# Residual rows turned for the router, token lists in halves, and seven and eight weight buffers in a two-layer hybrid decoder step

## The reference

```python
def hier_moe(h, w_group, b_group, w_router, b_router, w_gate, w_up, w_down):
    x2 = h.reshape(m, d)                       # rms_norm(residual) * gain
    g_logits = x2 @ w_group + b_group
    g_w, g_idx = lax.top_k(jax.nn.softmax(g_logits, axis=-1), 1)
    e_in = (x2 @ w_router + b_router).reshape(m, N_GROUPS, E_PER_GROUP)[jnp.arange(m), g_idx[:, 0]]
    top_v, top_i = lax.top_k(e_in, TOP_K_INNER)
    top_w = jax.nn.softmax(top_v, axis=-1) * g_w
    combine = ...                              # top_w at the two chosen experts of each row
    for e in range(N_EXPERTS):                 # 16 experts, D_FF_E = 512
        hid = jax.nn.silu(x2 @ w_gate[e]) * (x2 @ w_up[e])
        y = y + combine[:, e:e + 1] * (hid @ w_down[e])
```

## Time and profile before

| | before |
|---|---|
| median of 3 runs (lowest, highest) | 1469.57 us (1468.09, 1473.25) |
| the profiled execution: time, span | 1469.94 us, 1468.2 us |
| mean granted clock of TensorE, share of full | 0.948 |
| busy share of the span: PE, PEld, DVE, ACT, POOL | 90%, 51%, 39%, 21%, 13% |
| moved by DMA, mean rate | 341.06 MB, 232 GB/s |
| expert weights, issued at line 533 | 96 loads of 2 MB |

### The profile page before, as it was taken

One profiled execution on the slowest core, in us unless ns is written; L12 is line 12 of the kernel. 1 busy time (PEld: TensorE's weight loads), 2 busy tenths in 40 slices (PEclk: granted clock), 3 DMA queues, 4 the chain that ended last, 5 costly groups with the idle time before them and its releaser, 6 DMA issues. The chain is left out here.

```text
span 1468.2 us, 27307 instructions
## 1 busy us (share of the span) xinstructions
PE 1318.9 (90%) x10905; PEld 741.6 (51%) x10906; DVE 577.3 (39%) x1435; ACT 304.2 (21%) x783; POOL 185.4 (13%) x469
## 2 busy tenths in 40 slices
PE   7999999999599999887899998889995999998990
PEld 3444456544365456554643444556543655555550
DVE  2159944443423111111658995665216131111115
...
GB/s 283 193 132 58 147 315 314 340 123 131 182 324 264 393 376 403 405 409 359 105 0 58 33 115 116 116 116 73 216 72 174 196 320 366 397 391 402 403 268 205
DMA packets 87597, 341.06 MB, mean 232 GB/s; under 512 B 25843, under 2 KB 33107, under 8 KB 73506
## 3 DMA queue, kind: packets, MB, share of 16 engines
...
## 5 line engine op out<-in xcount | busy, mean ns | idle before, releaser
L1265 PE MATMUL banks<-arena 128*32 128x128 f32 (+1 forms) x4736 | 358.2, 334 | 26.7 <-issue 13.7
L1265 PEld LDWEIGHTS banks<-arena 128*32 128x32 f32 (+1 forms) x4736 | 238.9, 126 | 145.3 <-issue 52.5
L1293 PE MATMUL banks<-arena 128*64 128x512 f32 (+1 forms) x1184 | 173.1, 492 | 1.1 <-ACT arena L1755 1.1
L1861 DVE TENSOR_TENSOR arena<-arena,banks 128x256 f32<-128x256 f32 (+5 forms) x84 | 38.5, 459 | 272.1 <-PE banks L1265 176.8
L940 PE MATMUL banks<-arena 128*128 128x512 f32 x320 | 141.1, 595 | 1.2 <-DMA arena<-in_wstream 1.1
L2233 DVE COPY arena<-banks 128x256 f32<-128x256 f32 (+1 forms) x56 | 21.4, 382 | 295.8 <-PE banks L1278 289.5
L1861 DVE TENSOR_TENSOR arena<-banks,arena 128x512 f32<-128x512 f32 (+5 forms) x159 | 70.6, 473 | 124.4 <-ACT arena L1677 84.5
L1168 PE MATMUL banks<-arena 128*128 128x512 f32 x256 | 115.6, 610 | 3.6 <-ACT arena L1795 2.3
L968 PE MATMUL banks<-arena 128*128 128x512 f32 x256 | 116.5, 600 | 0.0
L1755 ACT ACTIVATE arena<-banks 128x512 f32<-128x512 f32 (+1 forms) x56 | 29.6, 528 | 363.2 <-PE banks L1293 363.2
L1293 PEld LDWEIGHTS banks<-arena 128*64 128x64 f32 (+1 forms) x1184 | 58.6, 123 | 84.4 <-issue 70.0
...
## 6 DMA issues: line engine op xcount, KB each, us to landing
...
```

Of the source, the lines that this page charges most:

```text
L1265: last = mm(bank(b, 0, 4 * n, n * j, n * j + n), x[:, c, :], w[:, c, 4 * n * j:4 * n * j + 4 * n], start=(c == 0), stop=(c == DC - 1))
L1293: last = mm(bank(3, 0, 8 * n, n * q, n * q + n), ht2[g % 2][:, 128 * i + n * j:128 * i + n * j + n], w[:, c, 8 * n * q:8 * n * q + 8 * n], ...
L1861: return v.tensor_tensor(out, x, y, op)
```

## The change

Four things change together.

- **Buffers.** The sets of three become one ring of seven slots in layer 0 and eight in layer 1: the three ring buffers, the three of `over_w`, then `WORK` 0 to 4096, and in layer 1 `QT` 0 to 4096. Block n goes to slot n mod 7 (8), and waits for the last product with block n-7 (n-8). `WORK` held the normed rows `hn`, so SP's loop waits for their transfers too.
- **Residual rows turned.** Norms 1 and 3 join `SCALED_LATER`: TensorE turns `h` itself, one job earlier in the order, and VectorE scales the logits. `hn` is still made, for the gathers, the last two tiles of it after all tiles are in `xt`. ScalarE's first copy of router sums moves ahead of its last root, and its load of the Exp table behind the copies.
- **Routing.** The weights of the choice go behind the lists (`choice_weights`); `slot_of` is made in two halves, each with its signal; the lists are copied and cast ahead of keys and rank.
- **First expert.** Its rows are copied in two halves, the first as soon as four of eight turns are done, and its gate product waits for the halves one by one.

Some semaphores are merged (`lf_dve`, `lf_act` to `lf`; `ln_var`, `ln_root`, `ln_done` to `ln`), with the same order.

```diff
-SCALED_LATER = (2,)
+SLOTS = (7, 8)
+SCALED_LATER = (1, 2, 3)
...
-    slots = [[[ring[2], ring[0], ring[1]], over_w], [[ring[1], ring[2], ring[0]], over_w]]
+    slots = [[ring[i] for i in first] + over_w + [at(*wide) for wide in more]
+             for first, more in (((2, 0, 1), [("WORK", 0, 4096)]), ((1, 2, 0), [("WORK", 0, 4096), ("QT", 0, 4096)]))]
...
+    def slot_of_block(l, s, i):
+
+        return slots[l][(3 * s + i) % SLOTS[l]]
+
+    def block_landed(l, s, i):
+
+        n = 3 * s + i
+        return f"weights{l}_{n % SLOTS[l]}", 16 * (n // SLOTS[l] + 1)
+
+    def block_used(l, s, i):
+
+        before, j = divmod(3 * s + i - SLOTS[l], 3)
+        name = ("gate_mm", "up_mm", "down_mm")[j] + str(l)
+        return name, upto(name, ENDS[before])
+
...
             sp.wait_ge(S(f"ranked{l}"), upto(f"ranked{l}", 1))
+            sp.wait_ge(S(f"hn_out{l}_0"), upto(f"hn_out{l}_0", 48))
+            sp.wait_ge(S(f"hn_out{l}_1"), upto(f"hn_out{l}_1", 32))
             for s in range(2, NE):
                 k = sp.value_load(block_i[0:1, s:s + 1], min_val=0, max_val=3 * NE - 3)
-                for i, name in enumerate((f"gate_mm{l}", f"up_mm{l}", f"down_mm{l}")):
-                    sp.wait_ge(S(name), upto(name, ENDS[s - 2]))
+                for i in range(3):
+                    if 3 * s + i >= SLOTS[l]:
+                        name, count = block_used(l, s, i)
+                        sp.wait_ge(S(name), count)
                     sp.wait_ge(S("x_in_0"), 16)
                     weights(l, s, i, a["wstream"][bass.ds(k + (b + i), 1)].rearrange("a p w -> (a p) w"))
 
...
                     last.then_inc(S(f"out_mm{l}"), 1)
+                    if b == 1 and t >= 1:
+                        turn_h(2 * l + 1, t - 1)
                     if b == 1 and t >= 2:
-                        turn_h(2 * l + 1, t - 2)
-                    if b == 1 and t >= 3:
-                        route_strips(l, t - 3)
-            turn_h(2 * l + 1, 3)
-            route_strips(l, 2)
+                        route_strips(l, t - 2)
             turn_h(2 * l + 1, 4)
             route_strips(l, 3)
             route_folds(l, (0, 1, 2), 1)
...
-            pe.wait_ge(S(f"placed{l}"), upto(f"placed{l}", 1))
             for n in range(2 * NT):
+                if n % NT == 0:
+                    pe.wait_ge(S(f"placed{l}"), upto(f"placed{l}", n // NT + 1))
                 last = mm(bank(5, 0, NE), slot_of[:, n, :], tok_of[:, n, :], start=(n == 0), stop=(n == 2 * NT - 1))
             last.then_inc(S(f"list_mm{l}"), 1)
...
+                if s == 0 and c == 3:
+                    last.then_inc(S(f"xg_used{l}"), 1)
...
+            def first_tokens(c):
+                if c % 4 == 0:
+                    pe.wait_ge(S(f"xgt{l}"), upto(f"xgt{l}", c // 4 + 1))
+
             pe.wait_ge(S(f"tok{l}"), upto(f"tok{l}", 1))
             turn_x(l, 0)
...
-                part_features(0, g3(slots[l][s % 2][0], DC), x, n).then_inc(S(f"gate_mm{l}"), 1)
+                part_features(0, g3(slot_of_block(l, s, 0), DC), x, n, first_tokens if g == 0 else None)\
+                    .then_inc(S(f"gate_mm{l}"), 1)
...
                 square(t)
+                if n % 2 and t == NT - 1:
+                    route_part(n // 2, 0)
                 if n in (2, 4):
                     if t:
...
+            route_part(l, 1)
+            route_part(l, 2)
             af(tick[2], tick[2], ACT.Exp)
...
                 if b == 1 and t >= 1:
-                    mean_square(2 * l + 1, t - 1)
-                    inverse_root(2 * l + 1, t - 1)
-                    normed(2 * l + 1, t - 1)
-                if b == 1 and t >= 2:
-                    to_xt(2 * l + 1, t - 2)
+                    to_xt(2 * l + 1, t - 1)
+                if b == 1 and t < NT - 1:
+                    mean_square(2 * l + 1, t)
+                    inverse_root(2 * l + 1, t)
+                if b == 1 and t < NT - 2:
+                    normed(2 * l + 1, t)
+            to_xt(2 * l + 1, NT - 1)
             mean_square(2 * l + 1, NT - 1)
-            to_xt(2 * l + 1, NT - 2)
             inverse_root(2 * l + 1, NT - 1)
+            normed(2 * l + 1, NT - 2)
             normed(2 * l + 1, NT - 1)
-            to_xt(2 * l + 1, NT - 1)
...
-            tt(logits[:, 0:4, :], g3(bank(1, 0, 80), 4), bc_mid(bv, 4), ALU.add)
-            tt(logits[0:64, 4, :], bank(1, 80, 100, 0, 64), bv[0:64], ALU.add).then_inc(S("dve_chain"), 1)
-            dve.wait_ge(S("dve_chain"), chained())
+            step(tt(logits[:, 0:4, :], g3(bank(1, 0, 80), 4), bc_last(rstd[:, 0:4], 20), ALU.mult))
+            v.scalar_tensor_tensor(out=logits[0:64, 4, :], in0=bank(1, 80, 100, 0, 64), scalar=rstd[0:64, 4:5],
+                                   in1=bv[0:64], op0=ALU.mult, op1=ALU.add)
+            step(tt(logits[:, 0:4, :], logits[:, 0:4, :], bc_mid(bv, 4), ALU.add))
...
             tt(sm[4][:, 0:NT], v2, v1, ALU.subtract).then_inc(S(f"route_dve{l}"), 1)
+            tt(tok_of.rearrange("p (k t) e -> p k t e", k=2), oh_both.rearrange("p k (t e) -> p k t e", t=NT),
+               tokid16[:, 0:NT].unsqueeze(1).unsqueeze(3).broadcast_to([128, 2, NT, NE]), ALU.mult)
+            dve.wait_ge(S(f"pos_mm{l}"), upto(f"pos_mm{l}", 1))
...
+            step(v.tensor_reduce(pos_of, some.rearrange("p (n e) -> p n e", e=NE), X, ALU.add))
+            for k in range(2):
+                tt(slot_of[:, NT * k:NT * k + NT, :], bc_mid(slot16, NT), bc_last(pos_of[:, NT * k:NT * k + NT], 128),
+                   ALU.is_equal).then_inc(S(f"placed{l}"), 1)
+            step(v.tensor_scalar(pos_x, pos_of, -float(CAP), None, ALU.add))
+            tt(slot_x, bc_mid(slot16[:, 0:32], 2 * NT), bc_last(pos_x, 32), ALU.is_equal).then_inc(S(f"extra{l}"), 1)
+            dve.wait_ge(S(f"list_mm{l}"), upto(f"list_mm{l}", 1))
+            v.tensor_copy(tok_f, bank(5, 0, NE))
+            v.tensor_copy(tok_u[:, 0:2], bank(5, 0, 2)).then_inc(S(f"tok{l}"), 1)
+            step(v.scalar_tensor_tensor(out=key, in0=cnt, scalar=16.0, in1=kofs, op0=ALU.mult, op1=ALU.add))
+            step(tt(g3(square, NE), bc_mid(key, NE), bc_last(key, NE), ALU.is_gt))
...
+            v.tensor_copy(block_i, block_f[0:1, :]).then_inc(S(f"ranked{l}"), 1)
+            list_order(l)
+            choice_weights(l)
+
+        def choice_weights(l):
+
             dve.wait_ge(S(f"route_act{l}"), upto(f"route_act{l}", 1))
...
-            tt(tok_of.rearrange("p (k t) e -> p k t e", k=2), oh_both.rearrange("p k (t e) -> p k t e", t=NT),
...
-            tt(slot_of, bc_mid(slot16, 2 * NT), bc_last(pos_of, 128), ALU.is_equal).then_inc(S(f"placed{l}"), 1)
...
-            step(tt(g3(square, NE), bc_mid(key, NE), bc_last(key, NE), ALU.is_gt))
-            step(v.tensor_reduce(rank, g3(square, NE), X, ALU.add))
-            dve.wait_ge(S(f"list_mm{l}"), upto(f"list_mm{l}", 1))
-            v.tensor_copy(tok_f, bank(5, 0, NE))
-            v.tensor_copy(tok_u[:, 0:2], bank(5, 0, 2)).then_inc(S(f"tok{l}"), 1)
-            step(tt(chosen, bc_mid(rank, NE), bc_last(rho, NE), ALU.is_equal))
...
-            v.tensor_copy(block_i, block_f[0:1, :]).then_inc(S(f"ranked{l}"), 1)
...
+            def first_half(k):
+                n = 32 * UNITS[0]
+                tt(xgt[0][:, 4 * k:4 * k + 4, 0:n], g3(bank(4 + k), 4)[:, :, 0:n],
+                   bc_last(gain[2 * l + 1][:, 4 * k:4 * k + 4], n), ALU.mult).then_inc(S(f"xgt{l}"), 1)
...
-            list_order(l)
-            inputs(0)
+            for half in range(2):
+                dve.wait_ge(S(f"xg_used{l}"), upto(f"xg_used{l}", half + 1))
+                first_half(half)
```

98 lines of the change are left out of this document (49 added, 49 removed).

## The result

The changed kernel took 1447.69 us in the median of four runs (1441.72 to 1448.93), the kernel before 1471.26 (1468.09 to 1473.25): a ratio of 0.9844, 95% interval 0.9819 to 0.9869, 23.6 us less. The forecast was 1445, its range 1437 to 1455. The profiled execution took 1448.93 us, 21.0 less than that of before.

A forecast was written before the change was run, and what follows sets the result against it. Expert stages were taken as bound by TensorE first, then by the weight stream, with a serial piece ahead of each. Gains of 9.0 (layer 0) and 16.1 us (layer 1), together 25.1, off 1469.94 gave about 1445 us, range 1437 to 1455.

The forecast's parts named there:

- Part 1, layer 0: Layer 0's expert stage: a seventh weight buffer puts the weight stream one block time earlier, gain 5.3 us.
- Part 1, layer 1: Layer 1's expert stage: seventh and eighth weight buffers put the weight stream two block times earlier, gain 12.4 us.
- The block would land 10.6 us earlier: Layer 1's last expert stall: its block lands at 1381.9 us, TensorE could be there at 1380.8, so 1.1 stays.
- A stall of about 3 us or more costs twice: Expert stages: the 32 matmuls behind such a stall run at lower clock, 5.18 and 5.36 us instead of 3.67.
- Part 2: Output projection to logits: turning residual rows without waiting for norms gains 1.3 us a layer; scaling logits loses 0.25.
- hops: Allowance between VectorE's steps from last residual sum to logits, bringing their summed 5.3 us to 5.7.
- Part 3: Routing on VectorE: weights of the choice moved back (0.6 us), copy and cast ahead of keys (1.0); 1.6 a layer.
- SP's loop waits in addition for the stored normed rows, which POOL waits for ahead of the first gather already: Routing, SP's loop: an added wait for stores that POOL already awaits before the first gather; no cost was given.
- Part 4: First expert: VectorE copies the first half of its rows while TensorE turns the second; 1.05 us a layer.
- The late gather: Rival: loads issued at the ranking delay each layer's first gather by up to 5.3 us, 1455 us; chance 0.08.
- Marked outcomes: What the new profile should show in expert stages and routing: waits, DMA work, first ranked load, logits and first product.
- signs of being wrong: Old-size stalls at later blocks, first gather over 5 us, or VectorE still at choice weights when first turned rows arrive.

The follow-up runs named there:

- before_again: The kernel before the change executed once more, nothing changed, to see how much its stretches vary; 1468.83 us.
- late_turns: The changed kernel with TensorE's turnings of row tiles and their logits' strips one output product later, as before, still turning residual rows; 1443.08 us.
- weights_before_lists: The changed kernel with the weights of the choice back ahead of the lists on VectorE; 1450.64 us.

## Why the prediction was right, point by point

The total held, 1447.7 for 1445, and the sign and both halves were right. That it held so closely is in part luck: by stretches, two terms fell 5.0 us short together and one came out 2.2 us larger. The terms, by the means above:

- *Part 1, layer 0: right.* 5.3 forecast, 5.7 measured.
- *Part 1, layer 1: the mechanism right, the size off.* 12.4 forecast, 9.8 measured. The failed step is "The block would land 10.6 us earlier", and with it the 1.1 us of stall that was to stay. The product behind the last stall began 250.6 us after the first product before, 242.1 after: 8.5 earlier. Without the stalls, TensorE would have been there at 238.8, so 3.4 of stall stayed, with its slow matmuls (5.36 us for 32, as in the earlier trace rows). The DMA engines did the 10.2 us of extra work ahead of the full stretch, and the lead was there: counted from the first product, a load that landed at 137.7 us before landed at 127.5, one of 185.2 at 175.6. Later one of 232.6 landed at 224.4, so some 2 us of the lead are lost between 176 and 224 us; to what is open. The Trainium skill, DMA: Bandwidth & Descriptors, section Where 436 GB/s comes from, has the HBM side bind at about 358 GB/s and would have made the term larger, not smaller; the trace disagrees again (392 to 399 GB/s in the full stretches shown).
- *"A stall of about 3 us or more costs twice": not borne out.* Three rows were too few. The kernel before itself has a stall of 3.59 us without slow matmuls, and stalls of 2.2 to 3.6 us went either way (before_again). The two counted in layer 0 and the one in layer 1 were there, so the sums stand; that the last stall would lose or keep its 1.7 us could not be forecast from its length.
- *Part 2: mechanism right, undersized by 0.9.* The 5.7 from the sum to the logits were 4.90. The failed step is the pieces with their "hops": 1.97 us for both tiles into xt and 1.41 for both normed rows were 2.05 and 1.55 in the sum, and between them there was hardly an idle moment. In layer 1 the half of the projection to the cast shrank by 3.5 us, of which 1.3 lie behind the logits, so the part is worth 2.2 where I had 1.3. late_turns shows that about 1.05 of it is the order on TensorE; that the rest is the norm no longer waited for is my reading, which no experiment isolates.
- *Part 3: right up to the cast.* Logits to cast fell by 1.34, forecast 1.6 - 0.25 = 1.35, with 0.62 for the weights of the choice (weights_before_lists; forecast 0.6). "SP's loop waits in addition for the stored normed rows, which POOL waits for ahead of the first gather already" named the wait that then cost time, and I took it for free: it had had 9 us of cover (the last store landed at 1126.0, the gather was issued at 1134.95 in the timeline of before), and this change took it away.
- *Part 4: right.* 0.95 to 1.1 for 1.05.
- *The late gather came, by another door and cheaper.* I looked for it among the loads issued at the ranking, and priced it at a block. It was the load issued at the end of the logits' products. In layer 0 it went out 11.5 us ahead of the cast before and had landed (383.8) when the gather was issued; SyncE issues it some 9 us after the last output product in both kernels, while the cast comes 6 us sooner after that product, so it now goes out 5.8 us ahead of the cast. In layer 1 it went out at 1122.8 before, behind the last store, and at 1110.3 now, just ahead of the last two. Price 0.9 and 1.5 us. The Trainium skill, DMA: Bandwidth & Descriptors, section Queues, rings and completion order, lets queues share an engine packet by packet; by that I had estimated half a block. The trace agrees in kind: the gather lost a part of a block and not the whole.
- *Marked outcomes.* Waits of 7 to 10 us in layer 0: 8.2, hit. Under 2 in layer 1: 4.0, miss. DMA work 5 and 10 us earlier: 5.2 and 10.2, hit. First ranked load within 1 us of the ranking: issued 388.52 for a ranking that ends at 387.7, and in layer 1 at 1124.51 for 1123.6, hit. First product 6.4 us after the cast: 6.44 in layer 0, 8.02 in layer 1, a miss by the gather. Of the signs of being wrong one is there: layer 0 keeps a stall of the old size, 4.1 us at 201 us behind its first product, where the kernel before had 4.06 at the same place.

Sum by the means: 5.7 + 9.8 for the buffers; for the routing 3.9 and 3.6 to the cast and 0.95 behind it in each layer, less 0.9 and 1.5 for the gather, 7.0. That is 22.5 us, for 23.6 between the medians and 25.1 forecast: layer 1's buffers fell short by 2.6, the gather took 2.4, and part 2 gave 2.2 more in the two layers.
